# Two projection chunks and part of the key work moved between the two attention kinds of a three-mixer layer

## What is computed

```python
h = x @ w_in
sb_cols, mla_cols, rwkv_cols = jnp.split(h, [SB_COLS, SB_COLS + MLA_COLS], axis=-1)
o_sb = merge_heads(stick_breaking_attention(q, k, v))
o_mla = mla_mixer(mla_cols, mla_q_norm, mla_w_uq, mla_kv_norm, mla_w_ukv)
o_rwkv = rwkv7_mixer(rwkv_cols, ...)
mix = jnp.concatenate([o_sb, o_mla, o_rwkv], axis=-1) @ w_o
```

## Time and profile before

| | |
|---|---|
| median of 3 runs | 2424.88 us (2423.84 to 2427.85) |
| profiled execution's own time | 2425.5 us |
| its span | 2423.7 us |
| PE busy | 2334.2 us, 96% of the span |
| DVE, ACT, POOL busy | 1383.4, 981.0, 240.2 us |
| mean granted TensorE clock | 0.991 of full speed |
| layer 0's attention on PE | about 100 to 235 us |
| layer 1's attention on PE | about 838 to 972 us |

### The profile page before, as it was taken

The page is one execution under the profiler, slowest core; times in us unless marked ns, Lnnn a source line. Parts: engine busy times, 40 slices in busy tenths (PEclk is TensorE's granted clock), DMA queues, the critical chain, the costliest instruction groups (busy, mean ns, idle before and its releaser), DMA issues.

```text
span 2423.7 us, 35763 instructions
## 1 busy us (share of the span) xinstructions
PE 2334.2 (96%) x13448; PEld 1873.0 (77%) x13448; DVE 1383.4 (57%) x1936; ACT 981.0 (40%) x1507; POOL 240.2 (10%) x192
## 2 busy tenths in 40 slices
PE   8998999999999998999999999999999999999998
PEld 6775767888887775777888887777888888788887
DVE  4567767666545457767656546675443446543443
ACT  5545435323235545535323234564232233422332
POOL 0041210000022031311000012101000001000001
PEclk9999999999999999999999998999999999999999
DMA  4220014555432220014565421222332222232222
GB/s 159 78 76 12 20 54 145 193 193 193 144 104 78 87 70 27 19 37 140 192 196 192 157 98 59 87 83 93 99 100 95 95 95 70 79 99 98 97 95 87
DMA packets 68796, 248.33 MB, mean 102 GB/s; under 512 B 7632, under 2 KB 8144, under 8 KB 68688
## 3 DMA queue, kind: packets, MB, share of 16 engines
q1 hardware_dynamic: 68688, 246.85, 30.7%
HBM read 244.72 MB, written 2.10 MB: 102 GB/s over the span
## 4 chain that ended last, share of the span: by engine, by line
PE 84%; DVE 8%; ACT 5%; issue 3%; POOL 0%; DMA 0%; DVEq 0%; ACTq 0%; SPq 0%; POOLq 0%
PE dense L590 24%; PE dense L592 24%; PE dense L591 24%; PE aux L697 1%; ACT wh L1385 1%; DVE wl L2006 1%; PE aux L880 1%; PE aux L993 1%; PE aux L1004 1%; PE aux L1089 1%; PE dense L618 1%; DVE nt L2065 0%; ACT xh L1439 0%; PE aux L890 0%; PE aux L704 0%
## 5 line engine op out<-in xcount | busy, mean ns | idle before, releaser
L590 PE MATMUL dense<-xh,wh 128*128 128x512 f32 x1840 | 733.0, 398 | 27.9 <-DVE wl L2006 10.7
L1385 ACT ACTIVATE wh<-raw 128x1024 fp32r<-128x1024 f32 x346 | 366.7, 1060 | 962.5 <-PE dense L592 955.5
L592 PE MATMUL dense<-xh,wl 128*128 128x512 f32 x1840 | 718.7, 391 | 0.0
L591 PE MATMUL dense<-xl,wh 128*128 128x512 f32 x1840 | 718.6, 391 | 0.0
L2006 DVE TENSOR_TENSOR wl<-raw,wh 128x1024 fp32r<-128x1024 f32 x346 | 427.5, 1236 | 495.0 <-ACT wh L1385 493.4
L590 PEld LDWEIGHTS dense<-xh,wh 128*128 128x128 f32 x1840 | 347.0, 189 | 121.9 <-issue 23.1
L591 PEld LDWEIGHTS dense<-xl,wh 128*128 128x128 f32 x1840 | 346.9, 189 | 73.8 <-issue 4.3
L592 PEld LDWEIGHTS dense<-xh,wl 128*128 128x128 f32 x1840 | 346.7, 188 | 73.3
L590 PE MATMUL dense<-hidh,wh 128*128 128x512 f32 x928 | 363.6, 392 | 4.9 <-DVE hidl L2038 2.1
L591 PE MATMUL dense<-hidl,wh 128*128 128x512 f32 x928 | 361.9, 390 | 0.0
L592 PE MATMUL dense<-hidh,wl 128*128 128x512 f32 x928 | 361.8, 390 | 0.0
(11 more groups left out here) (393 smaller groups left out, 2404.2 us busy)
## 6 DMA issues: line engine op xcount, KB each, us to landing
raw<-stream SPq DMA_DIRECT2D x362, 512.0 KB, 3.4
mraw<-mod_stream SPq DMA_DIRECT2D x96, 512.0 KB, 4.3
x<-x_t SPq DMA_DIRECT2D x4, 512.0 KB, 6.8
y_t<-x SPq DMA_DIRECT2D x8, 256.0 KB, 2.0
cst<-consts SPq DMA_DIRECT2D x1, 993.0 KB, 9.2
band<-bands SPq DMA_DIRECT2D x1, 576.0 KB, 4.4
cond<-c_rows SPq DMA_DIRECT2D x1, 512.0 KB, 10.1
pv_next<-vecs SPq DMA_DIRECT2D x3, 82.5 KB, 4.4
```

Of the source, the lines that this page charges most:

```text
L590: pe.matmul(o, a, h, start=first, stop=False)
L591: pe.matmul(o, a, l, start=False, stop=False)
L592: return pe.matmul(o, b, h, start=False, stop=last)
L1385: act.activation(wh[:, slot].rearrange("p k m -> p (k m)"), raw[:, slot, :], ACT.Copy).then_inc(hi_done, 1)
```

## The change

- The first kind holds 9 chunks (72 triples, 4 or 5 in a unit), and the last two run in the second kind, 2 triples in each of units 16 to 23, between `scores` and `turn`. Chunk ends fall in units 1, 3, 5, 7, 8, 10, 12, 14, 15, 19 and 23. In units 19 and 23 ACT handles the end before `turned`, DVE after `weights` and before the results of key norms and bonuses.
- The chunks are reordered: r0, k0 to k3, r1 to r3, v0 to v3, so that POOL can form the keys earlier.
- Key norms 0 and 1 move into the first kind (units 11 and 13), into bank aux4, which is free since the results of pair 0 are parked; 2 and 3 are at units 19 and 20 in aux5. Bonuses 0 to 2 are at units 17, 18, 21 in aux5, bonus 3 at 24 in `dense0`.
- The maxima replace the squares in `decay` instead of going to `knorm`. Squares 2 and 3 wait until normed keys 0 and 1 are out.
- ACT parks the results of the first kind in f32 in the place of `vsb` (`park`, after pair 4 and unit 16) and splits them at units 24 and 25.
- `e1` lies over the queries and keys of the first kind, so the exponentials no longer wait for the last chunk and start at unit 16, not 17.

The hunks that only rename, and the matching order of the weight stream, are left out:

```diff
@@ -49 +49 @@
...
 C_KRV = (13,) + tuple(range(15, 26))
+KRV = (0, 4, 5, 6, 7, 1, 2, 3, 8, 9, 10, 11)
+KRV_SB = 9
 C_WO = 26
...
@@ -324 +326 @@
...
         bv = at("bv", [P, 4, S], sig_at)
-        e1 = at("e1", [P, 4, S], xh_at + 4 * 4 * S)
-        knorm = at("knorm", [P, 4, S], xl_at + 4 * 4 * S)
+        e1 = at("e1", [P, 4, S], front_at)
+        parked = [vsb[:, :, P * q:P * q + P] for q in range(2)]
...
@@ -478 +481 @@
...
         zbank = (aux[0], aux[1], aux[3])
-        KRV_PARTS = KT * (len(C_KRV) - 1)
         SB_UNITS = NU // 2
-        KRV_AT = [next(u for u in range(SB_UNITS)
-                       if (u + 1) * KRV_PARTS // SB_UNITS >= KT * (c + 1))
+        MLA_TRIPLES = 2
+        def krv_upto(u):
+            if u <= SB_UNITS:
+                return u * KRV_SB * KT // SB_UNITS
+            return min(KT * (len(C_KRV) - 1), KRV_SB * KT + (u - SB_UNITS) * MLA_TRIPLES)
+        KRV_AT = [next(u for u in range(NU) if krv_upto(u + 1) >= KT * (c + 1))
                   for c in range(len(C_KRV) - 1)]
...
         LORA_BANKS = (aux[4], aux[5], aux[2], aux[3])
-        KEYS_AT = (16, 17, 20, 21)
-        BONUS_AT = (18, 19, 22, 23)
-        ROOT_AT = (19, 23)
-        HATS = {18: "a0", 19: "a1", 20: "a2", 21: "a3 k0", 22: "k1 n0", 23: "n1 b0", 24: "b1 k2",
-                25: "k3 s0", 26: "n2 s1", 27: "n3 b2", 28: "b3 s2", 29: "s3 r0", 30: "r1 r2",
-                31: "r3"}
-        EXP_AT = range(17, 21)
+        KEYS_AT = {11: 0, 13: 1, 19: 2, 20: 3}
+        BONUS_AT = {17: 0, 18: 1, 21: 2, 24: 3}
+        KEY_BANK = (aux[4], aux[4], aux[5], aux[5])
+        BONUS_BANK = (aux[5], aux[5], aux[5], dbank[0])
+        HATS = {17: "n0", 18: "n1", 19: "a0", 20: "a1 b0", 21: "b1 k0", 22: "a2 k1", 23: "a3",
+                24: "s0 n2", 25: "n3", 26: "b2 k2", 27: "b3 k3", 28: "s1 s2", 29: "s3 r0",
+                30: "r1 r2", 31: "r3"}
+        EXP_AT = range(16, 20)
+        OUT_AT = {24: 0, 25: 1, 26: 2}
         MODS = 24
...
@@ -898 +909 @@
...
                     if i == 0 and e == 0:
-                        pe.wait_ge(mixl_ready, L * 8 + q - 1)
+                        pe.wait_ge(out_parked, L * 2 + q - 1)
+                        if q == 2:
+                            pe.wait_ge(ss_max, L * 4 + 2)
+                        else:
+                            pe.wait_ge(bonus_read, L * 4 + 3)
                     o = aux[4 + q % 2][64 * e:64 * e + 64, i * P:(i + 1) * P]
...
@@ -920 +935 @@
...
                     pe.wait_ge(kksq_ready, L * 4 + p + 1)
-                    if p < 2:
-                        pe.wait_ge(bank_free[p], pl.bank(C_WO, p))
+                    if p == 0:
+                        pe.wait_ge(out_parked, L * 2 + 1)
+                    elif p == 2:
+                        pe.wait_ge(bonus_read, L * 4 + 2)
                     else:
-                        pe.wait_ge(bonus_read, L * 4 + p - 1)
-                    pe.matmul(dbank[p % 2][:], const("heads"), decay[:, p % 2, :], start=True,
+                        pe.wait_ge(ss_max, L * 4 + p)
+                    pe.matmul(KEY_BANK[p][:], const("heads"), decay[:, p % 2, :], start=True,
                               stop=True).then_inc(ss_pe, 1)
...
                     pe.wait_ge(rkk_ready, L * 4 + p + 1)
-                    pe.wait_ge(ss_max, L * 4 + p + 1)
-                    pe.matmul(dbank[p % 2][:], const("heads"), rkb[:, p % 2, :], start=True,
+                    if p == 0:
+                        pe.wait_ge(out_parked, L * 2 + 2)
+                    elif p == 1:
+                        pe.wait_ge(bonus_read, L * 4 + 1)
+                    elif p == 2:
+                        pe.wait_ge(ss_max, L * 4 + 4)
+                    else:
+                        pe.wait_ge(bank_free[0], pl.bank(C_WO, 0))
+                    pe.matmul(BONUS_BANK[p][:], const("heads"), rkb[:, p % 2, :], start=True,
                               stop=True).then_inc(bonus_pe, 1)
...
@@ -952 +976 @@
...
                     turn(2 * j + 1)
+                    if 2 * j + 1 in KEYS_AT:
+                        key_norm(KEYS_AT[2 * j + 1])
                     krv_part(2 * j + 1)
...
                         scores(u + 2)
+                    krv_part(u)
                     turn(u)
...
                     if u in BONUS_AT:
-                        bonus(BONUS_AT.index(u))
+                        bonus(BONUS_AT[u])
                     if u in KEYS_AT:
-                        key_norm(KEYS_AT.index(u))
+                        key_norm(KEYS_AT[u])
                 values(NU - 1)
...
@@ -1576 +1603 @@
...
+                def park(q):
+                    act.wait_ge(av_done, L * NU + 8 * q + 8)
+                    act.activation(parked[q], aux[4 + q][:].rearrange("q (b t) -> q b t", b=BLOCKS),
+                                   ACT.Copy).then_inc(out_parked, 1)
                 def pair_out(q):
+                    if q < 2:
+                        act.wait_ge(pe_chunk, pl.chunk(C_WO))
+                        act.wait_ge(out_parked, L * 2 + q + 1)
+                        act.activation(xh[:, q, :].rearrange("q (b t) -> q b t", b=BLOCKS),
+                                       parked[q], ACT.Copy).then_inc(mixh_ready, 1)
+                        return
                     act.wait_ge(av_done, L * NU + 8 * q + 8)
...
                        .then_inc(mixh_ready, 1)
+                def root(n, step):
+                    if step == 0:
+                        act.wait_ge(ss_max, L * 4 + 2 * n + 2)
+                        act.activation(decay[:], decay[:], ACT.Ln).then_inc(kn_sd, 1)
+                    else:
+                        act.wait_ge(kn_sd, L * 4 + 2 * n + 1)
+                        act.activation(decay[:], decay[:], ACT.Exp, scale=-0.5).then_inc(kn_sd, 1)
+                def chunk_end(c):
+                    done(pl, C_KRV[c])
+                    keep_own(C_KRV[c], krv[:, KRV[c], :], KRV[c] + 2)
...
@@ -1592 +1646 @@
...
                         weights(2 * j + 3)
+                    else:
+                        root(0, 0)
+                    if j == 4:
+                        park(0)
                     for c in chunks_after(j):
-                        done(pl, C_KRV[c])
-                        keep_own(C_KRV[c], krv[:, c, :], c + 2)
+                        chunk_end(c)
                 for u in range(SB_UNITS, NU):
...
                         weights(u + 1)
+                    if u in KRV_AT:
+                        chunk_end(KRV_AT.index(u) + 1)
                     turned(u)
-                    if u in ROOT_AT:
-                        n = ROOT_AT.index(u)
-                        act.wait_ge(ss_max, L * 4 + 2 * n + 2)
-                        act.activation(knorm[:, 2 * n:2 * n + 2], knorm[:, 2 * n:2 * n + 2],
-                                       ACT.Ln).then_inc(kn_sd, 1)
-                    if u - 1 in ROOT_AT:
-                        n = ROOT_AT.index(u - 1)
-                        act.wait_ge(kn_sd, L * 4 + 2 * n + 1)
-                        act.activation(knorm[:, 2 * n:2 * n + 2], knorm[:, 2 * n:2 * n + 2],
-                                       ACT.Exp, scale=-0.5).then_inc(kn_sd, 1)
+                    if u == SB_UNITS:
+                        park(1)
+                        root(0, 1)
+                    if u == 22:
+                        root(1, 0)
+                    if u == 23:
+                        root(1, 1)
                     if u in EXP_AT:
...
                         if p == 0:
-                            act.wait_ge(pe_chunk, pl.chunk(C_WO))
                             act.wait_ge(cum_ready, L * 4 + 4)
...
                            .then_inc(exp_tile, 1)
-                    if u == 16:
-                        act.wait_ge(pe_chunk, pl.chunk(C_WO))
-                        pair_out(0)
-                    if u > 16 and u % 8 == 1:
-                        pair_out(u // 8 - 1)
+                    if u in OUT_AT:
+                        pair_out(OUT_AT[u])
                 pair_out(3)
...
@@ -2256 +2308 @@
...
                     dve.wait_ge(mixh_ready, L * 8 + q + 1)
+                    if q < 2:
+                        blocks = "q (b t) -> q b t"
+                        low(xl[:, q, :].rearrange(blocks, b=BLOCKS), parked[q],
+                            xh[:, q, :].rearrange(blocks, b=BLOCKS), mixl_ready)
+                        return
                     low(xl[:, q, :], aux[4 + q % 2][:], xh[:, q, :], mixl_ready)
+                def key_max(p):
+                    dve.wait_ge(ss_pe, L * 4 + p + 1)
+                    ts(decay[:, p % 2, :], KEY_BANK[p][:], 1e-12, None, ALU.max)\
+                        .then_inc(ss_max, 1)
+                def bonus_value(p):
+                    dve.wait_ge(bonus_pe, L * 4 + p + 1)
+                    tt(bv[:, p, :], BONUS_BANK[p][:], krv[:, 8 + p, :], MUL)\
+                        .then_inc(bonus_read, 1)
+                def chunk_end(c):
+                    refill(pl, C_KRV[c])
```

(42 more changed lines are left out.)

## The result

The changed kernel takes 2447.49 us, the median of 4 runs (2447.27 to 2449.01), against 2425.56 us for the kernel before in the same comparison: 21.9 us more. The ratio of the two sets of runs is 1.0086, 95% interval 1.0073 to 1.0099 (the quotient of the medians is 1.0090). The prediction was 2441 us, slower, in a range of 2428 to 2449, so the measured time lies inside it by 1.5 us, and 0.5 us above the 2434 to 2447 that the forecast itself was given. The profiled execution took 2447.27 us, its span is 2445.5. Medians and ratios leave out executions in the chip's slow state; there was one, of 3342.78 us, of `late_no_move` further down.

The account below looks back on a forecast made before the run. TensorE (PE) is busy for 96% of the span, so only its waits and lower clock matter. Waits +6.3 and clock +1.7 make +8.0 us a layer, +16 in all: 2441 us, slower, range 2428 to 2449.

Parts of the forecast that it names:

- The waits: PE's waits in one layer's attention, new ones less those removed or filled: +6.3 us a layer.
- Key norm 1: Unit 13, first kind: PE newly waits for DVE's key_max(0), queued behind weights 14 and 15; +4.4 us, bounds 0 and 5.5.
- Unit 16: Start of the second kind: two triples fill 1.4 of the 3.2 us wait behind a chunk's end; 1.8 us left.
- Unit 19: Key norm 2 newly waits for DVE's bonus 1 product behind chunk 10's end; +3.0 us, bounds 0.0 and 4.0.
- Unit 24: Turn 24 newly waits for DVE's weights behind chunk 11's end; +2.4 us, bounds 0 and 3.
- The start: First kind's first turn waits for DVE with 4 triples ahead, not 5; wait grows by +0.7 us.
- The bank's wait: First kind, at a chunk's start, where a bank is freed late: the wait goes, −1.0 us.
- The second half of the second kind: Units 24 to 31, paced by DVE: one more split, one hat fewer, 0; low clock unchanged, bounds −2 and +1.
- The clock: Low granted clock behind the wait at unit 13, before krv_part(13): +1.7 us a layer, bounds 0 and 2.
- rival 1: Waits of units 16, 19 and 24 each get their own slow stretch: +3.4 us a layer, 2448 us; chance 0.12.
- Rival 2: Units 19 and 24 don't wait since DVE or ACT runs ahead: +2.6 us a layer, 2430 us; chance 0.10.
- Rival 3: Triples fill the second kind, no new wait appears, including unit 13: −5.3 us a layer, 2414 us; chance 0.08.

Follow-up runs that it names:

- late_no_move: ends_late with all 11 chunks back in the first kind and no triples in the second: 2418.9 us, ratio 0.9968 to the kernel before.
- filled_wait: Changed kernel plus four f32 products of a constant, unread, in PE's wait at key norm 1: ratio 1.0069 to the kernel before.
- ends_late: both_first, with DVE also taking the last three chunk ends one unit later: ratio 0.9953 to the kernel before, 0.9954 (2415.12 us) on a second chip.
- bonus_first: Changed kernel, but in the second kind DVE takes results of key norm and bonus before a chunk's end: ratio 1.0052 to the kernel before.
- both_first: bonus_first plus DVE's key_max before the next units' weights in the first kind: ratio 1.0003 to the kernel before.

## Why the prediction was right, and where its size was off

*That work only moves, and the sum is waits and clock:* right. Layer 0 closes to 0.1 us in these two terms, layer 1 to 0.8.

*The waits* were forecast at +6.3 us a layer and came to +5.9. Key norm 1: forecast 4.4, measured 4.59. Unit 16: 1.8 and 1.80. Unit 19: 3.0 and 3.02. Unit 24: 2.4 and 2.18. The start: 0.7 more, and 3.82 for 3.16. The bank's wait went, as said. All of them could be worked out from the order of three engines' lists and rows of the kernel before. The second half of the second kind was costed at no change; turn 27 waits 1.35 us where 0.5 stood before, a small miss, and the wait of 0.5 us for ACT early in the first kind went, another, which cancels half of it.

*The clock* is the term that was mis-sized: +1.7 us a layer forecast, +5.0 and +5.1 measured. The stretch behind key norm 1 cost 1.6, as forecast. What I left out, in layer 0: the start's stretch cost 3.4 us where the whole first kind lost 1.7 before (in layer 1 it cost 1.7 in both kernels, so this part is the luck of an execution); unit 19's wait was followed by its own stretch (1.7), as unit 16's was before, but unit 24's came too, and from 222 us on 5.2 us were lost against 3.4. That is rival 1, nearly to its figure (2448, measured 2447.5), though not in its places: unit 16's wait of 1.8 us left the clock alone in this kernel, and the start made up for it. That the figure fits so well is partly luck. The waits were also 35.6 us apart (187.27 to 222.85), not within 20 us. The Trainium skill (TensorE: Matmul & The Clock Gate, Part 1) says that the gate follows how busy TensorE has been of late. The trace agrees as far as `filled_wait` goes, with the wait filled and the clock at 1.00.

The prediction said that both low stretches of the kernel before stand behind the longest waits, and that waits of about 1 us left the clock alone. That is not so for its third and costliest stretch, the 3.4 us of 216 to 235 us. It begins behind waits of 1.11 and 0.49 us:

```profile
219.96 0.44 PE L880 MATMUL aux<-cst,wts 128*128 128x128 f32 x2 [1.11 <-DVE wts L2225]
222.15 0.69 PE L880 MATMUL aux<-cst,wts 128*128 128x128 f32 x2 [0.49 <-DVE wts L2225]
...
222.00:224.00 2.00, 1.85 (x7) 1.19 (x8) 1.97 (x6) 0.93 (x4) 0.00 (x0) 0.50 0.00 0
```

In layer 1 of the same execution the same waits, of 1.11 and 0.49 us, had no such stretch behind them, and one of 1.12 us after them none either. So as much clock was lost behind several short waits as behind a long one, and in the other layer nothing.

*Rival 2* (units 19 and 24 don't wait) is refuted by their rows. *Rival 3* (the triples fill the idle time and nothing new waits) named the place that decides, key norm 1; `ends_late` comes near what it describes, by another order of DVE's list. It reaches 0.9953, some 11 us below the kernel before, where rival 3 gave 10.6 below. The terms are not the same ones, since rival 3 kept 1.8 us at unit 16, so that the two figures agree is in part luck.

## What to carry to other kernels

Before work is moved into idle time, list for each engine, in its own order, what stands ahead of every result that another engine waits for. Here a maximum of 0.7 us, placed behind 3.8 us of weights, and a product placed behind the end of a chunk cost more than the idle time was worth. Move first what others wait for, and put long housekeeping behind it: three such reorders turned +0.86% into −0.47%. Try such a reorder before any move: in the kernel before, one alone gave −0.31%. A wait amid dense matmuls should be costed with the slow stretch that may follow it, 1.7 to 3.4 us in these profiles, and not only with its own length. The table in the next section tells how often it did.

## What I had not expected of the hardware

The same wait does not always cost the same clock. The start of the first kind waits 3.8 us in the changed kernel and in `bonus_first`, with the same instructions up to there. The granted clock of 100 to 120 us is 0.83 in the first, 3.4 us lost, and 0.91 in the second, 1.8 lost. The two profiles of `ends_late` itself have 0.91 and 0.83. Likewise the 3.02 us wait at key norm 2 is followed by 0.86 in 202 to 214 us in the changed kernel, but in `filled_wait` the clock stays at 1.00 there, in 183 to 214 us:

```profile
183.00:203.00 20.00, 15.65 (x77) 10.02 (x78) 12.57 (x29) 11.14 (x27) 8.75 (x6) 1.00 0.17 53
203.00:214.00 11.00, 11.00 (x57) 7.67 (x56) 6.11 (x13) 4.11 (x10) 0.00 (x0) 1.00 0.01 2
```

Counted over both layers of all twelve profiles, this is how often a wait of a given length had a granted clock of 0.5 behind it, with 1.00 ahead of it:

| PE's wait | layers that have it | with a slow stretch behind |
|---|---|---|
| 4.59 us, key norm 1 | 6 | 6 |
| the same, filled with products (1.06 us idle) | 2 | 0 |
| 3.82 to 3.86 us, the start | 13 | 13 |
| 3.02 us, key norm 2 | 6 | 3 |
| 2.17 to 2.18 us, turn 24 | 10 | 8 |
| 1.80 us, turn 16 | 10 | 5 |

The waits, by contrast, repeat to a few hundredths of a microsecond from kernel to kernel at the key norms and at turns 16 and 24. The start's wait is an exception: 3.14 us in layer 0 of `both_first` and 3.84 in layer 1, with the same instructions. So a forecast can be sharp on waits behind a chain that it has traced, and should keep a band for each for the clock. What decides whether the clock falls behind a given wait stays open; no run here varied anything that would settle it.
